# A mixture-of-experts loop on one core: rounds of eight experts in place of four

## The reference, cut to what matters

```python
g_w, g_i = lax.top_k(g_prob, 1)                      # the best of 4 groups
e_w, e_i = lax.top_k(jax.nn.softmax(e_logits), 2)    # two of its 8 experts
weights = e_w / jnp.sum(e_w) * g_w
hg = jnp.einsum('nd,edf->nef', t, w_gate)            # 1024 -> 256
hu = jnp.einsum('nd,edf->nef', t, w_up)
y = jnp.einsum('nef,efd->nd', jax.nn.silu(hg) * hu * gates[:, :, None], w_down)
```

## Time and profile before

| what | before |
| --- | --- |
| median of three runs | 1239.99 us (1237.75 to 1240.44) |
| the profiled execution's own time | 1240.41 us |
| its span in the profile | 1238.7 us, 26144 instructions |
| mean granted TensorE clock | 0.953 of full speed |
| PE busy | 1126.9 us, 91% |
| DVE / ACT / POOL busy | 563.0 / 268.8 / 172.8 us |
| DMA | 314.19 MB, 254 GB/s in the mean |

### The profile page before, as it was taken

The page is one execution under the profiler, slowest core; times in us unless marked ns, Lnnn a source line. Parts: engine busy times, 40 slices in busy tenths (PEclk is TensorE's granted clock), DMA queues, the critical chain, the costliest instruction groups (busy, mean ns, idle before and its releaser), DMA issues.

```text
span 1238.7 us, 26144 instructions
## 1 busy us (share of the span) xinstructions
PE 1126.9 (91%) x9179; PEld 644.5 (52%) x9180; DVE 563.0 (45%) x1196; ACT 268.8 (22%) x648; POOL 172.8 (14%) x261
## 2 busy tenths in 40 slices
PE   6999979999888999999699999999998798999995
PEld 4644646654654555555456653344556454555553
DVE  1031265643543444444434235777455334444445
ACT  2211235631121222121222222221021211222221
POOL 0152120000121111211000001111011111112110
PEclk9999999999798999999899998998996989999998
DMA  9856899740998999999512211000139899987893
GB/s 361 310 186 225 280 327 327 269 131 4 374 358 337 404 422 423 421 421 391 211 68 83 87 69 68 0 1 0 71 104 361 333 376 374 420 346 286 334 423 159
DMA packets 82734, 314.19 MB, mean 254 GB/s; under 512 B 11160, under 2 KB 12097, under 8 KB 57321
## 3 DMA queue, kind: packets, MB, share of 16 engines
q1 hardware_dynamic: 77658, 300.56, 62.6%
q0 software_dynamic: 1952, 6.90, 1.6%
q10 hardware_dynamic: 3056, 5.77, 1.2%
HBM read 307.82 MB, written 5.39 MB: 253 GB/s over the span
## 4 chain that ended last, share of the span: by engine, by line
PE 83%; DVE 6%; DMA 4%; issue 4%; SPq 2%; ACT 1%; POOL 0%; ACTq 0%; POOLq 0%; DVEq 0%
PE banks L472 80%; DVE arena L1046 4%; DMA arena<-in_ada_b 3%; DMA arena<-token_rows,arena 1%; PE banks L669 1%; SPq L1961 1%; PE banks L764 1%; SPq L1959 1%; PE banks L888 0%; DVE arena L1196 0%; PE banks L615 0%; POOL arena L1849 0%; DVE arena L1206 0%; PE banks L523 0%; DVE banks L1046 0%
## 5 line engine op out<-in xcount | busy, mean ns | idle before, releaser
L472 PE MATMUL banks<-arena 32*128 32x256 f32 (+10 forms) x8752 | 1072.5, 415 | 78.9 <-issue 37.1
L472 PEld LDWEIGHTS banks<-arena 128*32 128x32 f32 (+5 forms) x8752 | 593.2, 153 | 533.3 <-issue 410.2
L1046 DVE TENSOR_TENSOR arena<-banks,arena 128x64 f32<-128x64 f32 (+3 forms) x282 | 113.2, 413 | 69.2 <-PE banks L472 63.4
L1046 DVE TENSOR_TENSOR arena<-arena 128x384 f32<-128x384 f32 (+12 forms) x239 | 138.8, 588 | 4.5
L1314 DVE SCALAR_TENSOR_TENSOR arena<-arena 128x768 f32<-128x768 f32 x81 | 84.4, 1042 | 107.3 <-issue 105.0
L1700 ACT ACTIVATE arena<-banks 128x512 f32<-128x512 f32 x79 | 47.2, 597 | 223.8 <-PE banks L472 222.2
L1856 POOL TENSOR_TENSOR arena<-arena 128x256 f32<-128x256 f32 x81 | 59.4, 733 | 260.3 <-PE banks L472 242.7
L1324 DVE TENSOR_SCALAR arena<-arena 128x64 f32<-128x64 f32 x79 | 15.8, 199 | 162.2 <-ACT arena L1704 162.2
L1882 POOL COPY arena<-arena 128x256 f32 x77 | 30.5, 397 | 155.8 <-PE banks L472 152.2
L1836 POOL TENSOR_SCALAR arena<-arena 128x8 f32<-128x8 f32 (+2 forms) x28 | 6.8, 244 | 315.7 <-ACT arena L1547 227.9
L1414 DVE TENSOR_SCALAR arena<-arena 128x385 f32<-128x385 f32 x24 | 11.6, 481 | 82.4 <-ACT arena L1761 82.4
(11 more groups left out here) (151 smaller groups left out, 446.8 us busy)
## 6 DMA issues: line engine op xcount, KB each, us to landing
arena<-in_moe_w_gate SPq DMA_DIRECT2D x64, 1024.0 KB, 8.2
arena<-in_moe_w_up SPq DMA_DIRECT2D x64, 1024.0 KB, 10.6
arena<-in_moe_w_down SPq DMA_DIRECT2D x64, 1024.0 KB, 10.9
arena<-in_ada_w SPq DMA_DIRECT2D x24, 2048.0 KB
arena<-in_hy_w_in SPq DMA_DIRECT2D x6, 2048.0 KB
arena<-in_attn_w_in SPq DMA_DIRECT2D x3, 2048.0 KB
arena<-mod_rows SPq DMA_DIRECT2D x8, 512.0 KB, 9.2
arena<-in_attn_w_out SPq DMA_DIRECT2D x2, 2048.0 KB
```

What stands on the lines that cost most here:

```text
L472: return pe.matmul(out, lhsT, rhs, start=start, stop=stop, skip_group_check=True)
L1046: return dve.tensor_tensor(o, p, q, op)
```

## The change

PE and ACT get rounds of eight experts. The place is e % 4, so an expert keeps its place, its weights and its turn; the counts that are waited for are the same numbers as before, now written as `used`. Four of the seven boundaries between rounds become boundaries between two experts inside a round. The written-out round 0 and the loop's body each hold eight experts in place of four, and the loop runs three times in place of seven. SP, DVE and GpSimd are not touched. For PE:

```diff
-                def four_experts(r, first):
-                    n, b = steps_of(pe, r * 4)
-                    for s in range(4):
-                        if not (first and s == 0):
-                            pe.wait_ge(gu_loaded[s], (r + 1) * 32 + l * 32 * (NE // 4))
-                        if first and s == 0:
+                def eight_experts(r, first):
+                    n, b = steps_of(pe, r * 8)
+                    for e in range(8):
+                        s, used = e % 4, r * 2 + e // 4 + 1
+                        if not (first and e == 0):
+                            pe.wait_ge(gu_loaded[s], used * 32 + l * 32 * (NE // 4))
+                        if first and e == 0:
...
-                        following = steps_of(pe, r * 4 + s + 1) if s < 3 else None
-                        pe.wait_ge(down_loaded[s], (r + 1) * 16 + l * 16 * (NE // 4))
+                        following = steps_of(pe, r * 8 + e + 1) if e < 7 else None
+                        pe.wait_ge(down_loaded[s], used * 16 + l * 16 * (NE // 4))
                         with pe.If_ne(pe.to_reg(n), 1):
                             with pe.Fori(1, n) as j:
                                 one_step(b + j, s, s)
-                        if s < 3:
+                        if e < 7:
                             n, b = following
 
-                four_experts(0, True)
-                with pe.Fori(1, NE // 4) as r:
-                    four_experts(r, False)
+                eight_experts(0, True)
+                with pe.Fori(1, NE // 8) as r:
+                    eight_experts(r, False)
```

and for ACT:

```diff
-                def four_experts(r, first):
-                    n, b = steps_of(act, r * 4)
-                    for s in range(4):
+                def eight_experts(r, first):
+                    n, b = steps_of(act, r * 8)
+                    for e in range(8):
+                        s = e % 4
                         gates(b)
-                        if not (first and s == 0):
+                        if not (first and e == 0):
                             rows_out(b, (s - 1) % 4)
                         sigmoid(b)
-                        following = steps_of(act, r * 4 + s + 1) if s < 3 else None
+                        following = steps_of(act, r * 8 + e + 1) if e < 7 else None
...
-                four_experts(0, True)
-                with act.Fori(1, NE // 4) as r:
-                    four_experts(r, False)
+                eight_experts(0, True)
+                with act.Fori(1, NE // 8) as r:
+                    eight_experts(r, False)
```

## The result

The changed kernel takes 1291.37 us (median of 4 runs, 1285.42 to 1293.21) against 1238.87 for the kernel before, measured beside it (4 runs, 1235.35 to 1240.44): a ratio of 1.0396, with an interval from 1.0355 to 1.0437. It is 4% slower. The profiled execution took 1290.89 us (span 1289.1), 50.5 more than that of before. The predicted 1304 is 12.6 us above the median, inside the range, and on the right side.

The account below looks back on a forecast made before the run. TensorE, busy 91% of the span, was taken to bound the kernel. From 1240.4 us, 5.1 gained at boundaries, 45 for first visits and refetches and 24 for jumps back gave 1304 us, range 1252 to 1348.

Parts of the forecast that it names:

- The bound and the mechanism: TensorE bounds the kernel; its doubled loop body no longer stays in the engine, so instruction blocks are fetched again.
- 103 were named: TensorE's instruction queue q8 was to carry about 103 packets, spread over both expert loops to their end.
- rival A: TensorE's loop body stays in the engine; only boundary gains and first visits count: 1250 us, chance 0.24.
- C: First visits cost nothing and the body stays; eight boundaries go and nothing is added: 1235 us, chance 0.09.
- B: Refetched code in the expert loops comes at its full price, as stalls lower the clock: 1349 us, chance 0.17.
- (e): Two jumps back per layer find their target gone: 6 us each, 24 in all, bounds 2.3 and 12 each.
- (c): First visits of 16 experts per layer instead of 8: 0 to 30 us, part of a joint 45.
- (d): TensorE's loop body may not stay, so experts 16 to 31 are refetched: up to 60 us, part of a joint 45.
- the heads: Slow start of each expert loop, experts 1 to 7, code's first visit: 7.26 and 8.00 us a step against 5.91 and 5.87.
- steps of 6.5 to 7.5 us throughout: Sign that the forecast is right: expert steps this long throughout, where a single step took 5.84 us before.
- (a): Four of seven round boundaries per layer go, eight in all, at 0.54 + 0.1 us each: 5.1 us gained.
- (b): ScalarE's same edit costs nothing, since its boundary work lies in time when it waits for TensorE.

Follow-up runs that it names:

- bodies of 1488 and 1744 instructions: Kernel before, with 24 and 40 never-executed matmuls added per expert in TensorE's loop body of four experts: 1265.81 and 1516.84 us.
- light weights: Changed kernel with the weight transfers for experts 4 to 31 of each layer cut to one short piece per matrix: 1240.75 us.
- The light kernel before: Kernel before with the weight transfers for experts 4 to 31 of each layer cut to one short piece per matrix: 1225.28 us.
- the kernel with four more first visits per layer: Kernel before with TensorE's written-out part holding eight experts and its loop body still four, six passes: 1241.04 us, ratio 0.997.

## Why the prediction was right, point by point

**The bound and the mechanism** held. Time added to TensorE's stream arrived whole. The body of eight experts does not stay; 111 packets came where 103 were named, since each of the four later passes takes 11 (50 + 17 + 4 x 11), not 9. That a body of 8.6 blocks would not stay was a choice between two cases that no row decided; the bodies of 1488 and 1744 instructions decide it, with 53 and 163 packets. The long gaps lie exactly behind experts 15 and 23 of each layer, and rival A, with 67 packets and 1250 us, is out, as are C and, by its 1349 us, B.

**(e) The jumps back** were sized at 6 us each, 24 in all. The bounds of 2.3 and 12 us, and the 6 us for request and packet in the upper one, were my estimates, and no row ahead of the runs shows them. The runs show 4.3 to 6.1 us from the start of the first packet to the next matmul, and stops of 4.41 to 5.69 us with light weights. The gaps measure 6.51 to 9.99 us, 30.5 above what stood there, and with the slow step behind each 39.4. Undersized: it left out that the clock falls in such a stop, and that the packet itself starts late, 2.0 to 4.0 us into the stop, which "a stop with the request on its way" did not suggest.

**(c) and (d) First visits and refetches** were sized at 45 us between 0 and 90. This was the step that failed. The whole rise less (e), at 39.4, is 11 us, of which 4.7 lie outside the loops. The kernel without a loop allows more, some 17 us and the boundaries that it saves. How the clock lost behind a stop is shared between jumps and first visits can't be told more closely. The price per expert came from the heads, 10.9 + 15.2 = 26 us for the first visits there. The light kernel before, in its one run, suggests that its experts lose some 17 us to the traffic altogether, and the kernel with four more first visits per layer shows no cost that can be measured. The heads hold clusters of stops (2.02, 2.72 and 3.07 us) that hardly repeat in the steady part of the changed kernel: its experts 12 to 31 show two, of 2.14 and 2.72 us. The DMA share doesn't tell the two apart: 0.90 and 0.96 in the heads, 1.01 and 0.87 behind them. Of the marks, "steps of 6.5 to 7.5 us throughout" is the one that is plainly wrong: most steps in the rounds behind took 5.57 us and a gap of about 0.5.

**(a) The boundaries** were sized at a gain of 5.1 us; it did not arrive. The two behind experts 11 and 27 of layer 0 still show 0.75 and 0.79. At the two behind expert 11 and expert 19 of layer 1, both experts with several steps, the gap is gone altogether. Over the six later ones (behind experts 11, 19 and 27 of both layers) I add up 4.9 us before and 2.5 after. But the ordinary gap between two single-step experts rose, from 0.29 to the 0.43 to 0.62 of the chain above. In experts 12 to 31 of both layers, with the places of the jumps and two stops of 2.14 and 2.72 us left out, the gaps sum to 12.7 us before and 14.8 after, although the four boundaries among them fell from 3.3 to 1.7. The trace's records of the branch over a second step show a part of it: taken, in code that stayed, it lasts 207 to 227 ns, in the changed kernel mostly 320 to 570. That took back what the boundaries gave. It was not among the terms.

**(b) ScalarE**: nothing, as measured alone.

In sum, -5.1 + 45 + 24 = +63.9 was forecast and about 0 + 11 + 39.4 = +50.4 came. A term four times too large, one too small by 15 us and a gain that stayed out partly made up for each other: that the sum came within 12.6 us was luck. The range held mainly because it kept the bounds of (c) and (d).

## What to carry to other kernels

Count the instructions of a loop body on the engine that bounds the kernel, in blocks of 256 (48 experts of 272 came with 51 packets; an fp32 call here leaves four instructions, 64 matmuls and as many weight loads for 32 calls), and add the block ahead: on TensorE eight blocks stayed and nine did not (53 and 163 packets). Below that line a longer round has at most some 0.5 us per boundary to save (gaps of 0.77 to 0.84 us against 0.29 to 0.36); above it each jump back of the changed kernel cost 6.5 to 10 us while weights streamed, and the clock with it (0.50 of full speed). Read it in the trace as packets of the instruction queue that keep coming behind a loop's first pass.

If a body doesn't fit, writing it out is better than looping over it: it beat the loop of eight by 2.6% here, though it is 1.3% behind the loop that fits.

## What had not been expected of the hardware

- The limit is sharp: 53 packets at eight blocks, 163 at nine; and 24 and 275 us more than the kernel before, with the same matmuls.
- Instruction packets wait behind weight traffic: no packet of q8 starts in the first 3.9 us of a stop with the DMA engines at 99%. With light traffic a jump stops TensorE for 4.4 to 5.7 us, not 6.5 to 10. Once the first packet has started, both take the same 4.3 to 6.1 us.
- A stop is paid twice. In each stop at a jump the granted clock went to 0.50, and the step behind took 7.18 to 8.45 us in place of 5.57.
- The same branch over a second step, taken, lasts 207 to 227 ns in code that stayed. In code that is fetched anew it is mostly 320 to 570 ns in the changed kernel and 320 to 440 in its light form, so the weights' traffic is not what makes it slow.
- The kernel with 24 never-executed matmuls per expert fetches only three packets more than before and loses 23.7 us beside its neighbour, with an idle time up by 24.6: five of its stops, 2.18 to 6.90 us, lie in the first pass of its loop, where it jumps over padding for the first time; by the trace's record the jump at the first of them took 5.46 us.
